# Cross-attention with its two weight products formed from memory alone, and HGRN2 pairs that project independently

## The reference, cut to what matters

```python
h = rms_norm(x, norm_mix)                      # x (1024, 1024)
p = h @ w_in                                   # 1024 -> 3904 columns, four head groups of 256
y = concat(rwkv7(p_a), conv(p_b), hgrn2(p_c), stick_breaking(p_d))
x = x + y @ w_out
hx, mn = rms_norm(x, norm_xattn), rms_norm(mem, norm_mem)      # mem (256, 1024)
q = (hx @ wq) per head;  k = (mn @ wk) per head;  v = (mn @ wv) per head    # 4 heads of 256
s = einsum('bthd,bmhd->bhtm', q, k) * 256 ** -0.5
p = softmax(s);  o = einsum('bhtm,bmhd->bthd', p, v)
x = x + o @ wo
out = rms_norm(x, norm_final)
```

## Time and profile before

| | us |
|---|---|
| median of 3 runs | 1282.67 (1282.64 to 1282.78) |
| the profiled execution, its own time | 1282.02 |
| its span, first to last instruction | 1279.9 |
| PE busy | 1120.5 (88%) |
| DVE, ACT, POOL busy | 580.1, 402.7, 314.7 |

### The profile page before, as it was taken

How to read it: one execution, slowest core, us unless ns; L and a number is a source line. 1 busy time by engine, 2 the same in 40 slices (tenths; PEclk the granted TensorE clock), 3 DMA queues, 4 the chain that set the end, 5 groups by cost and what they waited for, 6 DMA issues and landing times.

```text
span 1279.9 us, 25488 instructions
## 1 busy us (share of the span) xinstructions
PE 1120.5 (88%) x11104; PEld 940.3 (73%) x11104; DVE 580.1 (45%) x767; ACT 402.7 (31%) x668; POOL 314.7 (25%) x291
## 2 busy tenths in 40 slices
PE   4798999998999899999979533888899899898996
PEld 3576877776779677687757432777899788788996
DVE  4345276885963545537543535541413400254114
ACT  5314010235231255653345333222202411253004
POOL 1332012242420022131200001577442034300220
PEclk7799999998999899999989565899799999999998
DMA  5110000111110011011100002232521011100113
GB/s 192 49 33 18 19 19 19 35 35 32 34 35 4 2 34 34 17 42 26 35 1 1 1 1 91 75 92 75 197 70 48 2 50 55 61 2 1 34 34 132
DMA packets 71726, 55.45 MB, mean 43 GB/s; under 512 B 2944, under 2 KB 67520, under 8 KB 71616
## 3 DMA queue, kind: packets, MB, share of 16 engines
q1 hardware_dynamic: 71616, 53.83, 14.1%
HBM read 49.63 MB, written 4.19 MB: 42 GB/s over the span
## 4 chain that ended last, share of the span: by engine, by line
PE 66%; DVE 14%; ACT 12%; POOL 3%; issue 2%; DMA 2%; DVEq 0%; ACTq 0%; SPq 0%; POOLq 0%
PE bank L857 12%; PE bank L870 11%; PE bank L858 10%; PE bank L859 10%; PE bank L1141 4%; PE bank L1143 4%; PE bank L1142 4%; ACT B L1197 3%; DVE A L1476 3%; ACT A L1197 2%; DVE B L1777 2%; DVE yT L1479 2%; PE duo L1083 2%; POOL wlo L807 2%; PE duo L1096 2%
## 5 line engine op out<-in xcount | busy, mean ns | idle before, releaser
L857 PE MATMUL bank<-act_hi,whi 128*128 128x512 f32 (+1 forms) x752 | 307.2, 408 | 12.4 <-POOL wlo L807 10.2
L858 PE MATMUL bank<-act_lo,whi 128*128 128x512 f32 (+1 forms) x752 | 287.6, 382 | 0.0
L859 PE MATMUL bank<-act_hi,wlo 128*128 128x512 f32 (+1 forms) x752 | 287.4, 382 | 0.0
L806 POOL TENSOR_SCALAR whi<-wraw 128x512 fp32r<-128x512 f32 x94 | 72.7, 773 | 615.8 <-PE bank L859 581.7
L857 PEld LDWEIGHTS bank<-act_hi,whi 128*128 128x128 f32 x752 | 145.2, 193 | 53.4 <-issue 17.5
L870 PEld LDWEIGHTS bank<-A 64*64 64x64 f32 x4608 | 146.3, 138 | 35.7 <-issue 18.7
L870 PE MATMUL bank<-A 64*64 64x64 f32 x4608 | 156.4, 223 | 13.5 <-DVE A L1626 9.9
L859 PEld LDWEIGHTS bank<-act_hi,wlo 128*128 128x128 f32 x752 | 145.0, 193 | 29.7
L858 PEld LDWEIGHTS bank<-act_lo,whi 128*128 128x128 f32 x752 | 145.8, 194 | 25.4 <-issue 1.7
L1141 PE MATMUL bank<-vhi,act_hi 128*128 128x256 f32 x512 | 147.0, 287 | 8.0 <-DVE x L1797 3.0
L1143 PE MATMUL bank<-vhi,act_lo 128*128 128x256 f32 x512 | 145.7, 285 | 0.0
(11 more groups left out here) (150 smaller groups left out, 1324.8 us busy)
## 6 DMA issues: line engine op xcount, KB each, us to landing
wraw<-in_w_in SPq DMA_DIRECT2D x62, 256.0 KB, 2.8
A<-in_x SPq DMA_DIRECT2D x8, 512.0 KB, 3.6
vraw<-in_w_out SPq DMA_DIRECT2D x16, 256.0 KB, 2.9
x<-in_x SPq DMA_DIRECT2D x8, 512.0 KB, 7.6
wraw<-in_wq SPq DMA_DIRECT2D x16, 256.0 KB, 2.8
vraw<-in_wo SPq DMA_DIRECT2D x16, 256.0 KB, 2.6
out<-yT SPq DMA_DIRECT2D x8, 512.0 KB, 2.6
B<-in_wk SPq DMA_DIRECT2D x8, 256.0 KB, 2.8
```

Of the source, the lines that this page charges most:

```text
L806: done(pool, nc.gpsimd.tensor_scalar(hi, raw_view[slot], 1.0, 1.0, ALU.mult, ALU.mult), "w_hi")
L857: mm(bank, wh, act_hi[:, k, cols], start=k == 0, stop=False)
L858: mm(bank, wh, act_lo[:, k, cols], start=False, stop=False)
L859: ins = mm(bank, wl, act_hi[:, k, cols], start=False, stop=k == KT - 1)
```

## The change

It does five things.

1. **Products from memory.** The tiles `q` go. New tiles `qa` (8) form wq_h k_h^T: wq comes in transposed from the host, k (`k_hi`, `k_lo`, already scaled) is the moving side of 256 columns; 24 matmuls a tile. New tiles `vo` (8: four heads, two column halves each) form v_h wo_h with wo as the moving side of 512 columns; 12 matmuls a tile. Each result is copied by ACT to one of six slots (`moved`, `mem_raw`) and stored by SP to DRAM (`keys_dram`, `vals_dram`, 1024 x 1024 each).
2. **Attention.** `ascore`, `aturn`, `aval` and `vtr` go. `wide s` (hx times `keys_dram`) has the form of `wide o`: 4 x 8 x 24 matmuls. Its column group n is head n, so softmax works on 256 columns (`smax`, `snorm`). During n = 3 the probabilities of all heads are transposed (`pT`) and split; `wide f` multiplies them by `vals_dram`.
3. **Place of the memory work.** It has SBUF of its own (`mem_hi`, `k_hi`, `v_hi` and so on), and becomes a fourth chain of the planner: `mn` waits for `all_in`, no longer for the end of the stick chain, and `mk`, `mv`, `qa`, `vo` are filler pieces behind it.
4. **HGRN2.** Each pair has its own rows of `A` for q, k, z and att, so pair 1's tiles wait for `rfin(1)` only. The two sigmoids of f move from the tile's copy into `hgate`.
5. **Planner.** `HOLD` is empty; `SLACK` 0.38 to 0.4, `SLACK_OTHER` 0.32 to 0.5, `SUPPLY` 3.47 to 3.8, `SMALL_RUN` 1.57 to 1.0, `SMALL_PER_PIECE` 1.69 to 2.0.

The core of the diff:

```diff
-SLACK, SLACK_OTHER = 0.38, 0.32
-SUPPLY = 3.47
-HOLD = {('cmean',): ('gt', 1, 0),
...
+SLACK, SLACK_OTHER = 0.4, 0.5
+SUPPLY = 3.8
+HOLD = {}
...
     for w in "fqi":
-        want("h", 1, w, after=[("hfin", 0)])
+        want("h", 1, w, after=[("rfin", 1)])
...
+    mem = [(("mn", 0), [("AE", 1.7), ("D", 1.3)], all_in), (("mn", 1), [("AE", 1.7), ("D", 1.3)], []),
+           (("mT", 0), [("P", 0.9), ("A", 1.2), ("D", 1.4)], [("mn", 0)]),
+           (("mT", 1), [("P", 0.9), ("A", 1.2), ("D", 1.4)], [("mn", 1)])]
...
+    for n in range(KT):
+        want("qa", n, after=[("proj", "mk", KT - 1, 0)])
+    for hd in range(4):
+        for h in range(2):
+            want("vo", hd, h, after=[("proj", "mv", KT - 1, 0)])
...
-    chains, pieces = [list(rec), list(conv), list(stick)], [(("xw",), 1, k) for k in range(KT)]
+    chains, pieces = [list(rec), list(conv), list(stick), list(mem)], [(("xw",), 1, k) for k in range(KT)]
...
+    for n in range(4):
+        for i in range(TT + 2):
+            if i < TT:
+                s += [("wide", "s", n, i), ("smax", n, i)]
+            if 0 < i <= TT:
+                s.append(("snorm", n, i - 1))
+            if n == 3 and i > 1:
+                s.append(("pT", i - 2))
...
+                if tiles[n] == ["mk", 0]:
+                    for t in tiles[:n]:
+                        pj.rd_open(sp, tuple(t) + (1,))
+                    load_mem()
                 load_w(n)
-            load_wides(4, 8)
+                for j in range(2 * (n - 2 - first_move), 2 * (n - 1 - first_move)):
+                    if j >= 0:
+                        store(j)
+            for j in range(2 * (len(tiles) - 2 - first_move), 2 * (len(tiles) - first_move)):
+                store(j)
+            load_wides(0, 1)
+            mixers_done(sp)
...
+            load_wides(1, 12)
...
+                if kind[0] == "qa":
+                    if k == 0:
+                        pe.wait_ge(sem("w_split"), 2 * n + h + 1)
+                    e = 4 * h + k
+                    o, wh, wl = bank[:, k // 2 * M:(k // 2 + 1) * M], whi[:, n % 2, e, :], wlo[:, n % 2, e, :]
+                    mm(o, wh, k_hi[:, e, :], start=k % 2 == 0, stop=False)
...
+                    mm(bank, v_hi[:, e, m], wh, start=k == 0, stop=False)
+                    mm(bank, v_hi[:, e, m], wl, start=False, stop=False)
+                    ins = mm(bank, v_lo[:, e, m], wh, start=False, stop=k == 1)
...
             def ysplit(i):
                 if i == 0:
                     mixers_done(act)
-                    pj.rd_open(act, ("mv", KT - 1, 0))
+                    for t in tiles[-2:]:
+                        for h in range(2):
+                            pj.rd_open(act, tuple(t) + (h,))
+                    wait_stored(act, len(moves))
...
+            def smax(n, i):
+                u, key = n * TT + i, ("wide", "s", n, i)
+                bank = pj.rd_open(dve, key)
+                pj.rd_done(dve, V.tensor_reduce(soft[:, 0, u:u + 1], bank[:, 0:M], AX.X, MAX), key, nth=1)
+                ts(soft[:, 1, u:u + 1], soft[:, 0, u:u + 1], -1.0, None, MUL, name="s_max")
```

More of the change, by code:

```diff
@@ L98, in weight_columns, with piece_list @@
     return "w_in", first + kind[1] * P
+def piece_list(kind):
+    if kind[0] in ("mk", "mv"):
+        return [(0, k) for k in range(KT)]
+    n = {"qa": 4, "vo": 2}.get(kind[0], KT)
+    return [(h, k) for h in range(2) for k in range(n)]
 def mixer_chains():
@@ L588, in program @@
                     so.plan(("o",) + a[:2])
[L589 to L596, removed]
+            elif name == "wide":
+                pj.plan((name,) + a, reads=2 if a[0] == "s" else 1)
+            elif name == "pT":
+                for q in range(2):
+                    tn.plan((name,) + a + (q,), reads=2)
         def run(table):
@@ L637, in two_heads @@
             return buf.rearrange("p (e s) -> p e s", e=2)[:, :, 0:w]
[L639 removed]
+        wides = [(w, n) for w in "osf" for n in range(4)]
         def wide_lo(m):
@@ L740, in load_wides @@
                             "(k p) n -> p k n", p=P)).then_inc(sem(f"v_loaded{u % 2}"), 16)
-            for n in range(1, len(tiles)):
[L743 to L755, removed]
-                    for i in range(2):
-                        sp.dma_start(B[:, 4 + i, :], mem[i * P:(i + 1) * P, :]).then_inc(sem("mem_loaded"), 16)
-                    sp.dma_start(B[:, 6, :], norms[NORM_MEM:NORM_MEM + 1, :].broadcast_to([P, D])).then_inc(
-                        sem("mem_loaded"), 16)
-                load_w(n)
@@ L778, in split_wides @@
             def split_wides(first):
-                for m in range(first, first + 4):
+                for m in range(first, len(wides)):
                     for q in range(4):
@@ L1116, in sbv @@
                     ins.then_inc(sem("av_done"), 1)
-            def vtr(n):
-                pj.wait_read(pe, ("mv", n, 0))
-                bank = pj.pe_open(pe, ("vtr", n))
-                for mi in range(2):
-                    ins = tr(bank[:, mi * P:(mi + 1) * P], kv_vt(n)[:, mi * P:(mi + 1) * P], ident)
-                pj.pe_post(ins, ("vtr", n))
             def wide(name, n, i):
@@ L1367, in hgate @@
             def hgate(p):
+                for h in range(2):
+                    pj.wait_read(act, ("h", p, "f", h))
+                if p:
+                    act.wait_ge(sem("h_done"), p)
+                done(act, av(A[:, hx, :], A[:, hz[p], :], ACT.Sigmoid), "hf_sig")
+                done(act, av(A[:, hk[p], :], A[:, hz[p], :], ACT.Sigmoid, scale=-1.0), "hf_sig")
                 act.wait_ge(sem("hf_floor"), p + 1)
@@ L1463, in _ @@
                  "mu": mu, "var": var, "csq": csq, "cvar": cvar, "cfin": cfin, "hgate": hgate, "hlev": hlev,
[L1464 to L1466 removed]
+                 "hbars": hbars, "hout": hout, "hvar": hvar, "sv": sv, "sbz": sbz, "sbt": sbt,
+                 "ysplit": ysplit, "x2n": x2n, "hT": lambda i: hi_part("hT", i),
+                 "pT": lambda i: hi_part("pT", i, tn), "smax": smax, "fin": fin})
         @block.vector
@@ L1841, in _ @@
                  "hlev": hlev, "hbars": hbars, "hkv": hkv, "hout": hout, "hfin": hfin, "sbz": sbz, "sbo": sbo,
-                 "ysplit": ysplit, "wide": wide, "x2n": x2n, "hT": lambda i: lo_part("hT", i), "ascore": ascore,
-                 "aval": aval, "fin": fin})
+                 "ysplit": ysplit, "wide": wide, "x2n": x2n, "hT": lambda i: lo_part("hT", i),
+                 "pT": lambda i: lo_part("pT", i, tn), "smax": smax, "snorm": snorm, "fin": fin})
 _OUT = ((1, T, D), "float32")
```

412 lines of the change are left out of this document (200 added, 212 removed).

## The result

| | before | after |
|---|---|---|
| median | 1282.66 us | 1245.55 us (1244.58 to 1245.96) |
| ratio | | 0.971 [0.969, 0.973] |
| span of the profiled execution | 1279.9 | 1244.1 |
| PE / DVE / ACT / POOL busy | 1120.5 / 580.1 / 402.7 / 314.7 | 1110.9 / 603.1 / 396.1 / 382.0 |

A forecast was written before the change was run, and what follows sets the result against it. The prediction took PE to bound the kernel nearly everywhere, with a hole at 720 to 795 us. Span 1279.9 - 64 - 52 + 6.5 + 4 = 1174.4 us, so a median of 1177 us; range 1146 to 1212.

The forecast's parts named there:

- Step 1: After 1011 us, `q` and attention go and `wide s` comes: 64 us gained (56 to 67).
- Step 2: Memory work grows and moves beside the mixers' chains; last memory matmul at about 843 instead of 894.55: 52 us gained.
- The first rival: Memory stage: POOL's splits held up by DVE, a tile taking 7.5 us, 43 us later, 1220 us; chance 15%.
- Step 3: Hand-over from memory tiles to `wide o`: w_out loads stand behind the last stores, 6.5 us lost (0 to 12).
- Step 4: HGRN2 pairs free of each other, sigmoids in `hgate`: worth nothing by itself, sigmoids within 3 us either way.
- Step 5: `HOLD` emptied and other slacks, reordering the first 565 us: 4 us lost, bounds a gain of 8 and loss of 20.
- The "mixers lose by the new order" rival: Before 669 us the new order loses 20 us or more, stick chain late as well: 1200 us; chance 12%.

The follow-up runs named there:

- the old order: The changed kernel with the planner constants and HOLD table of the kernel before (part 5 undone): 1221.72 us, ratio 0.952.
- the kernel with the old order and split levels: The changed kernel with the old constants and HOLD table, and each HGRN2 level's ACT and DVE half made its own planner stage: 1211.31 us, ratio 0.944.
- The split of the levels: The changed kernel with the ACT and DVE part of each HGRN2 level made a planner stage apart from its matmuls: 1245.49 us, ratio 0.970.
- the shorter splits: The changed kernel with levels split in two stages, POOL forming the low part of the 32 memory tiles for a quarter of the columns only: 1226.27 us.

## Why the prediction went wrong

**Step 1 (attention) was right.** `wide s` took 1140.08 - 1036.67 = 103.4 us for 101.2; the joint stalls PE by 2.31 + 0.95 us where I took 2.5; `smax` and `snorm` are hidden. The fp32 attention of 165.2 us is gone; 62 of the 64 us came. `wide o` takes 109.2 us to the first `wide s` matmul, and took 106.1 from 905.18 before; this is no growth, since 18 of its matmuls stood ahead of 905.18 (from 898.73 it took 112.5). But these 3 us were missing in the sum.

**Step 2 failed, on what runs beside what.** It had HGRN2 pair 1 inside the memory stage, and the stage over at 843. The runs show one or the other. With the old order the stage ends at 841.11, POOL's first split at 688.52 (forecast 687) and the stick chain's end at 833.66 (818 to 837) come true too, but pair 1's levels are outside and cost 58.8 us behind it. With the levels inside, it ends at 876.49. So the 841 agrees in part by luck: the work in it was less than forecast. POOL's price was not the error: 136.18/32 = 4.26 us a tile busy beside the mixers, in the kernel with the old order and split levels, where I took 4.75 with the gaps. Three assumptions failed.

- *That pair 0's chain would be over at `all_in`, and pair 1's chain lie beside the memory tiles.* Pair 0 ended at 726, 45 us after the memory load, and pair 1's levels were put behind everything. I had read in the code that a stage is taken only if PE idles for at most `SLACK`, but not asked what this rule does to a stage that needs ACT and DVE ahead of PE while another chain is always ready. The trace of before had the same order: pair 1's gate scan at 707.27, its level products only from 793.44, behind the end of the stick chain (777.27), and products of its end still at 847.24. I read those on POOL's account alone. This is the step that missed the 40 us: 56.7 from the last memory matmul to `wide o`.
- *That work moved beside other work is free.* The split of the levels took these 50 us out of the tail and gained nothing in the new order and 10 us in the old one. The moved products of DVE took up to 1.9 times as long beside POOL (831 to 448 ns), the memory tiles came later, and the waits for w_out's splits, which the levels had hidden, showed (13.7 us). The first rival had the mechanism with the other loser: POOL lost little (in after from 700 to 872 low splits of 1.39 and 1.42 us on the mean, high ones of 0.80 and 0.69, for 1.27 and 0.62 alone). DVE lost, also in the scans of the stick chain (128x512: 1676 ns in after from 741 to 872, 1269 ns in before from 700 to 778, with POOL idle). That is 4 us for ten scans, and little of why the chain ended at 859 and not at 818 to 837. Most is its late start: its first exponent is at 691.95, where I had 672, and from there it took 168 us (forecast 146 to 165). Rows of before and of after:

```profile
L1777 DVE TENSOR_TENSOR_SCAN B<-fcst,B 128x512 f32<-128x512 f32 x8 | 10.2, 1269 | 0.3
```

```profile
L1802 DVE TENSOR_TENSOR_SCAN B<-fcst,B 128x512 f32<-128x512 f32 x10 | 16.8, 1676 | 0.4
```

  DVE's operations with one input from PSUM (`duo`) were not slowed: the next row is of the same stretch of after, and 1.22 us is what they took in before. By the Trainium skill ("SBUF — State Buffer", section "SBUF: two separate sides"), whichever of the two starts first holds the shared ports for its whole instruction, and on DVE's side this concerns, outside its 2-port modes, work with two SBUF inputs while GpSimd reads SBUF. The trace agrees as to the second; which of the two started first in each case was not read.

```profile
L1497 DVE SCALAR_TENSOR_TENSOR B<-duo,B 128x1024 f32<-128x1024 f32 x5 | 6.1, 1224 | 35.2 <-ACT B L1221 35.2
```

- *The time of `all_in`:* 681 and not 669, of which the old order gives back 8. The first split followed at 700.50 (forecast 687). Then POOL's 32 tiles took 168 us from first to last split, where I had 152: POOL stood 10.6 us in one wait, from 709 us on, with both weight buffers full, until PE had run `mk` 0, beside batches of pair 0's chain.

**Step 3 (hand-over) can't be read in after,** where the levels hide it. In the kernel with the old order and split levels it stands open. From the last memory matmul to the end of `wide o` (the first matmul of `q` or `wide s`) it took 125.1 us, before 116.7: 8.4 lost, where I took 6.5. Two loads moved ahead of the stores made it 121.5.

**Step 4 (freedom of HGRN2), "worth nothing by itself":** right only in that it acts through step 2. Taken away, it costs 41 us.

**Step 5 (the planner's constants) was the term sized worst.** 4 us taken as a loss, with 20 as the bound; measured are 24 in the changed kernel and 88 in the kernel before. I argued that reordering full work costs little. PE was indeed about as busy before 565 us (519 us, before 521). But the order decides what is *left* when the filler runs out: at the memory load pair 0 had 45 us to go in after, and had been over for 9 us in the kernel with the old order (664.24 and 673.62).

**The chances.** The "mixers lose by the new order" rival (12%) gave 1200 and ended its loss at 669 us. What came true together (order, tail of levels, slower products) stood in no rival, since each took one loss at a time.

**A correction.** The account of the change says that the memory work has SBUF of its own. Its tensors are placed where `act_hi` and `act_lo` have been given back, so they share addresses with x's split rows. So `mn` has to wait for `all_in`. An earlier start, which would give POOL its 136 us of splits earlier, was not tried.

**Open.** Why the old order gains 10 us from the split levels and the new order none (both uncover the same 13.7 us of waits for w_out); how the 19 us of the shorter splits divide between POOL's length and DVE's waits; how much of the 39 us by which split levels delay the memory tiles is PE's order, and how much DVE's slower work.

## What to carry to other kernels

When work is moved into a hole, list by name and start time what else is still unfinished there, and ask of each item when the scheduler will let it run; a hole filled on PE only moves the end to the chain that was passed over. A greedy list scheduler that ranks stages by the idle time of one engine can starve stages that begin on another; splitting such a stage where it changes engine was worth 100 us in one kernel here, 10 in another and nothing in a third, according to what shared the stretch. And a change of planner constants is a change of its own: time it apart from the edit it comes with.

## What the runs showed of the hardware

POOL's splits and DVE's operations with two SBUF inputs slow each other, and not evenly: 128x256 products 448 ns beside a little of POOL's work, 831 beside full splits, 501 beside splits with a quarter of the low part; scans of 128x512 1269 ns with POOL idle and 1676 beside it; operations of 1024 columns with one input from PSUM 1224 ns in both; POOL's low split 1.27 us alone and 1.4 on the mean beside the mixers' DVE work, but 2.11 for each of the four while DVE splits y in one unbroken row of eight. An engine's busy time is therefore no constant to be moved from one stretch to another.
